# A two-layer decoder trunk on one core: the last expert quad in larger pieces with fillers, one early row block, and the residual through identity products

## The reference, cut to what matters

```
def hier_moe(h, w_group, b_group, w_expert, b_expert, w_in, w_out):
    ...
    def expert_block(args):
        xb, e = args
        hu = xb @ w_in[e]
        return (jax.nn.silu(hu[:, :EXPERT_FF]) * hu[:, EXPERT_FF:]) @ w_out[e]
    ...
```

## Time and profile before

| | |
|---|---|
| median of 3 runs | 1163.95 us (1163.62 to 1163.96) |
| profiled execution, its own time | 1165.64 us |
| its span, first to last instruction | 1163.8 us |
| mean granted PE clock | 0.865 |
| PE busy | 823.4 us, 71% of the span |
| DVE, ACT, POOL busy | 276.2, 140.6, 24.0 us |
| read from memory | 444.41 MB, 384 GB/s over the span |

### The profile page before, as it was taken

The page is one execution under the profiler, slowest core; times in us unless marked ns, Lnnn a source line. Parts: engine busy times, 40 slices in busy tenths (PEclk is TensorE's granted clock), DMA queues, the critical chain, the costliest instruction groups (busy, mean ns, idle before and its releaser), DMA issues.

```text
span 1163.8 us, 12340 instructions
## 1 busy us (share of the span) xinstructions
PE 823.4 (71%) x5238; PEld 403.2 (35%) x5238; DVE 276.2 (24%) x504; ACT 140.6 (12%) x328; POOL 24.0 (2%) x27
## 2 busy tenths in 40 slices
PE   9999999672727282818689999959191919190966
PEld 8965655130303030303234565613030303030322
DVE  3565673010101010101038746401010101010102
ACT  2011211010101010101012241101010101010100
POOL 1000110000000000000002100000000000000000
PEclk9999999895959595959789999989595959596989
DMA  9995398999999999999999818899999999999997
GB/s 351 274 330 214 152 389 344 429 432 425 435 423 430 429 433 427 433 425 426 416 416 405 346 71 344 336 429 432 427 431 427 435 424 432 427 433 427 425 419 286
DMA packets 46344, 447.74 MB, mean 385 GB/s; under 512 B 3632, under 2 KB 5976, under 8 KB 26072
## 3 DMA queue, kind: packets, MB, share of 16 engines
q1 hardware_dynamic: 44224, 444.42, 91.4%
q10 hardware_dynamic: 2072, 2.62, 1.2%
HBM read 444.41 MB, written 2.62 MB: 384 GB/s over the span
## 4 chain that ended last, share of the span: by engine, by line
PE 45%; DMA 43%; SPq 9%; issue 1%; DVE 1%; ACT 1%; POOL 0%; DVEq 0%; POOLq 0%
PE ps L1386 44%; DMA ring<-in_moe_w_in 40%; SPq L461 5%; SPq L378 4%; DMA spare<-in_moe_w_out 3%; PE ps L1389 1%; DMA xs<-in_x 0%; ACT ps L665 0%; DVE work L1133 0%; DVE ring L1265 0%; ACT work L661 0%; POOL rstd L518 0%; ACT work L608 0%; DVEq L65 0%; ACT work L753 0%
## 5 line engine op out<-in xcount | busy, mean ns | idle before, releaser
L1386 PE MATMUL ps<-ring,work 128*32 128x512 f32 (+1 forms) x2464 | 440.3, 651 | 298.3 <-DMA ring<-in_moe_w_in 286.8
L1386 PEld LDWEIGHTS ps<-ring,work 128*32 128x32 f32 (+1 forms) x2464 | 149.1, 132 | 564.6 <-issue 560.4
L1386 PE MATMUL ps<-work 128*32 128x512 f32 (+3 forms) x1170 | 214.1, 534 | 18.9 <-DVE work L1216 9.8
L1208 DVE SCALAR_TENSOR_TENSOR work<-work,ps 128x512 f32<-128x512 f32 x16 | 17.3, 1081 | 635.4 <-ACT work L691 635.4
L1386 PEld LDWEIGHTS ps<-work 128*32 128x32 f32 (+2 forms) x1170 | 88.5, 139 | 135.7 <-issue 111.3
L1386 PE MATMUL ps<-spare,work 128*32 128x512 f32 x256 | 117.1, 608 | 0.0
L691 ACT ACTIVATE work<-ps 128x512 f32<-128x512 f32 x16 | 17.5, 1097 | 539.3 <-PE ps L1386 539.3
L1386 PEld LDWEIGHTS ps<-work,xs 128*128 128x128 f32 x512 | 58.8, 192 | 15.1 <-issue 15.1
L1386 PE MATMUL ps<-work,xs 128*128 128x128 f32 x512 | 62.8, 279 | 0.0
L1386 PE MATMUL ps<-work,ring 128*128 128x128 f32 (+1 forms) x352 | 53.3, 313 | 0.3 <-DVE work L809 0.3
L1386 PEld LDWEIGHTS ps<-work,ring 128*128 128x128 f32 x352 | 49.3, 191 | 4.5 <-issue 0.6
(11 more groups left out here) (155 smaller groups left out, 353.2 us busy)
## 6 DMA issues: line engine op xcount, KB each, us to landing
ring<-in_moe_w_in SPq DMA_DIRECT2D x38, 4096.0 KB, 30.6
ring<-in_moe_w_in SPq DMA_DIRECT2D x44, 2048.0 KB, 14.2
work<-in_moe_w_out SPq DMA_DIRECT2D x42, 2048.0 KB, 34.8
spare<-in_moe_w_out SPq DMA_DIRECT2D x14, 2048.0 KB, 46.2
ring<-in_moe_w_in SPq DMA_DIRECT2D x16, 1024.0 KB, 30.3
ring<-in_hg_w_in SPq DMA_DIRECT2D x7, 2048.0 KB, 22.7
work<-in_moe_w_out SPq DMA_DIRECT2D x21, 512.0 KB, 17.6
ring<-in_w_kv SPq DMA_DIRECT2D x3, 2048.0 KB, 26.8
```

The costliest lines, as they stand in the source:

```text
L1208: dve.scalar_tensor_tensor(hid_rows, hid_rows, 1.0, in_hidden(6), ALU.add, ALU.mult).then_inc(silu_ready, 1)
L1386: return pe.matmul(o, l, r, start=start, stop=stop)
```

## The change

1. `load_last_up` has two pieces instead of three: row blocks 0 to 3 and 4 to 7. PE takes them so, with the 12 fillers after the first piece instead of after the second and third.
2. `load_last_down` has the pieces k 0 and 1, k 2, k 3 instead of four single k (in layer 1 the last is still cut into halves), and PE runs 12 fillers after the first and after the second piece.
3. After the up products of the last quad PE adds the residual to the four accumulators, by products of `ident` with it. At the end of a layer what is left is a copy of each accumulator: tile 0 by ACT (`sum_experts`, counted by the new `moe_summed`), tile 1 by DVE.
4. Row block 0 of the second quad's first expert is sent ahead, to `early` in region 5, after the last residual add and behind the opening loads; ACT copies it to its place in `ring` when PE has read the first quad's first row block. The refill's first part then has three experts. DVE waits for that copy before it writes in region 5.
5. `biasload` and `biasout` become one semaphore.

```diff
-ROW_PARTS = (1 + GRP, 2 + GRP)
+ROW_PARTS = (1 + GRP, 2)
+LAST_DOWN = (slice(0, 2), slice(2, 3), slice(3, 4))
...
+        early = rt[:, 896:1920]
...
+        def residual(layer, a, half):
+            if layer:
+                return x_rows[:, a, :, half * 64:(half + 1) * 64].rearrange("p k q -> p q k")
+            return x_rows[:, a, 4 * half:4 * half + 4, :].rearrange("p k q -> p q k")
...
@@ SP: load_opening, load_refill
+                    sp.wait_ge(x_added, 6 * (layer + 1))
+                    sp.dma_start(early, up_matrix(layer, GRP)[:, 0:D]).then_inc(early_in, 16)
...
-                        sp.dma_start(pairs[:, :, ns], source[:, :, ns]).then_inc(row_part_in[min(part, 1)], 16)
+                        xs = slice(0 if part else 1, GRP)
+                        sp.dma_start(pairs[:, xs, ns], source[:, xs, ns]).then_inc(row_part_in[min(part, 1)], 16)
...
@@ SP: the last quad
-                    for part, ks in enumerate(((0, 4), (4, 6), (6, 8))):
-                        if part == 1:
+                    for part, ks in enumerate(((0, 4), (4, 8))):
+                        if part:
                             sp.wait_ge(up_done, 2 * (P0 + QUADS - 1))
                         for x in range(GRP):
-                            load_pair(E - GRP + x, x, loaded[2 * x] if part == 2 else row_part_in[part], ks)
+                            load_pair(E - GRP + x, x, loaded[2 * x] if part else row_part_in[0], ks)
...
-                    parts = [(k, slice(0, D)) for k in range(KF)]
+                    parts = [(k, slice(0, D)) for k in LAST_DOWN]
                     if layer:
-                        parts[KF - 1:] = [(KF - 1, slice(0, 512)), (KF - 1, slice(512, D))]
+                        parts[-1:] = [(LAST_DOWN[-1], slice(0, 512)), (LAST_DOWN[-1], slice(512, D))]
...
@@ ACT: before the quads
+                act.wait_ge(early_in, 16 * (layer + 1))
+                act.wait_ge(first_k_done, 2 * layer + 1)
+                act.copy(pair(0)[:, 0:D], early).then_inc(early_moved, 1)
                 act.wait_ge(gat_done, 2 * P0 + 2)
                 weighted_columns(layer, 1, 1).then_inc(xg_ready, 2)
...
+            def sum_experts(layer, half):
+                act.wait_ge(c_done, 4 * (layer + 1) * QUADS - 3 + 2 * half)
+                if layer == 0:
+                    act.copy(x_rows[:, 0, 4 * half:4 * half + 4, :], ps[:, half, :].rearrange("p (q k) -> p k q", k=4))\
+                       .then_inc(moe_summed, 1)
+                else:
+                    act.copy(x_out[:, 0, half * 512:(half + 1) * 512], ps[:, half, :]).then_inc(moe_summed, 1)
...
@@ DVE
                 passes(layer)
+                dve.wait_ge(early_moved, layer + 1)
...
+                dve.wait_ge(c_done, 4 * (layer + 1) * QUADS - 2 + 2 * half)
+                if layer == 0:
+                    dve.tensor_copy(x_rows[:, 1, 4 * half:4 * half + 4, :], in_rows(ps[:, 2 + half, :])).then_inc(moe_added, 1)
+                else:
+                    dve.tensor_copy(x_out[:, 1, half * 512:(half + 1) * 512], ps[:, 2 + half, :]).then_inc(moe_added, 1)
...
@@ PE: the last quad
-                                for part, ks in enumerate((range(0, 4), range(4, 6), range(6, 8))):
-                                    if part < 2:
-                                        pe.wait_ge(row_part_in[part], 16 * ROW_PARTS[part] * (layer + 1))
+                                for part, ks in enumerate((range(0, 4), range(4, 8))):
+                                    if part == 0:
+                                        pe.wait_ge(row_part_in[0], 16 * ROW_PARTS[0] * (layer + 1))
                                     else:
                                         pairs_in()
...
-                                        if part == 2:
+                                        if part:
                                             i.then_inc(up_done, 1)
                                     if part == 0:
                                         i.then_inc(rows_done, 1)
-                                    if part:
                                         keep_busy(12, 5)
...
                             pe.wait_ge(xg_ready, it * (2 * UN) + (2 * q + 4))
+                        else:
+                            for a in range(TT):
+                                for half in range(2):
+                                    mm(ps[:, 2 * a + half, :], ident, residual(layer, a, half), False, False)
                         pe.wait_ge(hid_ready, it * UN + (q + 1))
...
-                        for k in range(KF - 1):
-                            pe.wait_ge(down_part_in[k], 16 * GRP * (layer + 1))
+                        for i, ks in enumerate(LAST_DOWN[:-1]):
+                            pe.wait_ge(down_part_in[i], 16 * GRP * (layer + 1))
                             for half in range(2):
-                                down(layer, down_home, half, [k])
-                        pe.wait_ge(down_part_in[KF - 1], 16 * GRP * (layer + 1))
+                                down(layer, down_home, half, range(KF)[ks])
+                            keep_busy(12, 5)
+                        pe.wait_ge(down_part_in[len(LAST_DOWN) - 1], 16 * GRP * (layer + 1))
                         down(layer, down_home, 0, [KF - 1]).then_inc(down_done, 1)
```

More of the change, by code:

```diff
@@ L192, in build @@
         ms_ready, rstd_ready, eps_added = sem("ms_ready"), sem("rstd_ready"), sem("ffn_eps_added")
-        x_added, moe_added = sem("residual_added"), sem("experts_added")
+        x_added, moe_added, moe_summed = sem("residual_added"), sem("tile1_experts_added"), sem("tile0_experts_added")
         row_part_in = [sem(f"row_part{i}_in") for i in range(2)]
-        down_part_in = [sem(f"last_down_part{k}_in") for k in range(KF)]
+        down_part_in = [sem(f"last_down_part{k}_in") for k in range(len(LAST_DOWN))]
         count_done = sem("counts_done")
@@ L447, in load_last_up @@
                 def load_last_up():
-                    for part, ks in enumerate(((0, 4), (4, 6), (6, 8))):
-                        if part == 1:
+                    for part, ks in enumerate(((0, 4), (4, 8))):
+                        if part:
                             sp.wait_ge(up_done, 2 * (P0 + QUADS - 1))
                         for x in range(GRP):
-                            load_pair(E - GRP + x, x, loaded[2 * x] if part == 2 else row_part_in[part], ks)
+                            load_pair(E - GRP + x, x, loaded[2 * x] if part else row_part_in[0], ks)
                 def load_last_down():
                     sp.wait_ge(down_done, 2 * (P0 + QUADS - 1))
-                    parts = [(k, slice(0, D)) for k in range(KF)]
+                    parts = [(k, slice(0, D)) for k in LAST_DOWN]
                     if layer:
-                        parts[KF - 1:] = [(KF - 1, slice(0, 512)), (KF - 1, slice(512, D))]
-                    for i, (k, cs) in enumerate(parts):
+                        parts[-1:] = [(LAST_DOWN[-1], slice(0, 512)), (LAST_DOWN[-1], slice(512, D))]
+                    for i, (ks, cs) in enumerate(parts):
                         for x in range(GRP):
-                            sp.dma_start(down_view(down_home[x])[:, k:k + 1, cs],
-                                         down_rows(moe_w_out[layer, E - GRP + x])[:, k:k + 1, cs])\
-                              .then_inc(down_in[x] if i == KF else down_part_in[i], 16)
+                            sp.dma_start(down_view(down_home[x])[:, ks, cs],
+                                         down_rows(moe_w_out[layer, E - GRP + x])[:, ks, cs])\
+                              .then_inc(down_in[x] if i == len(LAST_DOWN) else down_part_in[i], 16)
                 over_quads(sp, body, lambda: over(layer))
@@ L702, in moe @@
                 over_quads(act, body, lambda: over(layer))
+            def sum_experts(layer, half):
[5 more added lines that the diff above has]
+                    act.copy(x_out[:, 0, half * 512:(half + 1) * 512], ps[:, half, :]).then_inc(moe_summed, 1)
             moe(0)
+            for half in range(2):
+                sum_experts(0, half)
             act.wait_ge(down_done, 2 * QUADS)
@@ L779, in _ @@
             moe(1)
+            for half in range(2):
+                sum_experts(1, half)
         @block.vector
@@ L1360, in _ @@
             column_difference(MIX1 + 6, OUT_SUMS[1], out_quarter)
[L1361 removed]
+            dve.wait_ge(bias_moved, 2 * 16)
             for h in range(H + 1):
@@ L1785, in body @@
                                 if is_int(it, 0):
+                                    pe.wait_ge(early_moved, layer + 1)
                                     pe.wait_ge(row_part_in[0], 16 * (ROW_PARTS[0] * layer + 1))
@@ L1835, in columns_T @@
             def columns_T(half, a):
-                pe.wait_ge(moe_added, 2 * half + a + 1)
+                pe.wait_ge(moe_added if a else moe_summed, half + 1)
                 for k in range(4 * half, 4 * half + 4):
```

17 lines of the change are left out of this document (9 added, 8 removed).

## The result

The changed kernel takes **1177.55 us** (median of 4 runs, 1176.0 to 1177.71) against 1163.88 (1163.62 to 1163.96): ratio 1.0117, 95% interval 1.0104 to 1.013, so slower, and 0.55 us above the top of the forecast's range. The profiled execution took 1177.52 us (span 1175.7), 11.9 more than the one of before.

A forecast was written before the change was run, and what follows sets the result against it. An expert phase was taken to last as long as its weights' arrival plus PE's remaining work; 7.95 + 3.35 - 2.4 = +8.9 us gave 1174.5, less 1.7 for the median: 1172.8 us, range 1166.5 to 1177.

The forecast's parts named there:

- The mechanism: In each last quad, PE's work behind the last up weights, fillers included, sets the pace instead of the data.
- 27.3: Predicted microseconds from the last up weights to the last k in a last quad, a sum of seven PE terms.
- the term for the identity products: Last quad: four products adding the residual put at 5.6 us, between 3.70 and 6.9, by VectorE's add with steps.
- rival 2: Last quad: identity products cost 6.9 us by ACT's ratio, 1.3 more per layer, total 1175.4; chance 0.10.
- +8.9: Predicted net change in us: +7.95 second layer's end, +3.35 first layer, -2.4 for the early row block.
- dividing the final moves: End of layer 0: ACT takes two of four moves that followed each other on VectorE, put at -0.5 us.
- the 1.7 us taken off for the median: Final step: 1174.5 lowered to 1172.8 because the profiled execution of before lay 1.7 us above the median.
- 1: Rival, last quad: identity products cost 3.70 us as if read in sequence, 1.9 less per layer, 1169.0; chance 0.24.
- 3: Rival, last quad: clock stays up in PE's 7 us wait, 2.3 us less per layer, 1168.2; chance 0.10.
- 4: Rival, last quads: fillers and identity products stay inside waits, -8.3 us in total, 1155.6, faster; chance 0.09.
- 5: Rival, layer openings: the early row block brings nothing because the queue runs dry later, +2.4 us, 1175.2; chance 0.05.
- The sign: Whole kernel: the change makes it slower, chance 0.83, against 0.09 for faster and 0.08 for same.

The follow-up runs named there:

- e2: The changed kernel with the identity products reading the residual in sequence and the steps put on the accumulator's columns, same sum: 1170.95 us.
- e3: The changed kernel with no steps on either side of the identity products, so the residual is added to other columns: 1170.97 us.
- e9: The kernel before, unchanged, run again with one profiled execution: 1162.91 us.
- e10: The kernel before, unchanged, run once more with one profiled execution: 1164.03 us.
- e4: The kernel before with the early row block alone: 1161.89 us, ratio 0.9984.
- e5: The changed kernel without the two groups of fillers between the down pieces: 1164.97 us, ratio 1.0008.
- e8: The kernel before with the early row block and one group of 12 fillers per layer in the last quad's long wait: 1160.28 us.

## Why the prediction was right or wrong

**The mechanism was right.** PE's own work behind the last up weights became the bound, the fillers with it, without a wait for data. The clock was 0.50 when the up records began, as the text had it, and 1.00 from the identity products to the last k (585.80 to 605.50, and 1146.30 to 1166.00 in layer 1). In the recorded order, with the measured starts of layer 0 and layer 1: 64 up records 9.4 and 8.7 (put at 9.4); hidden rows 1.4 (1.2; the row of the identity products, 7.23 long, still runs in the first 0.2 of it); the first two k 3.6 (3.5); fillers 2.9, third k 1.85, fillers 2.9 (2.9, 1.75, 2.9). The chain came to 29.0 and 28.3 us for 27.3.

**The step that failed is the term for the identity products**: 5.6 us, by VectorE's add with steps, where PE took 7.05 and 7.0. That is rival 2's price (6.9, by ACT's ratio) and a little more; e2 and e3 show that the 512-byte steps of the moving operand are its cause. It makes +2.85 us, the bulk of the 3.0 by which the sum, +8.9, fell short of the +11.9 between the profiled executions. What remains is small and of both signs: dividing the final moves between ACT and DVE in layer 0 gave 0.1, not 0.5 (first sum to mark 5.12 before, 603.82 to 608.94, and 5.00 after, 608.45 to 613.45); the end of layer 1 became 0.5 shorter, not 0.3.

**The second step that failed is the last one**, the 1.7 us taken off for the median. The profiled execution of before lay above its median because its last k of layer 0, and to a small part the late k of layer 1, ran at the lower clock, as far as three executions show it (e9, e10). But the sum starts at the arrival of the last up weights, ahead of those blocks, and replaces them by a chain of PE's work at full clock. The changed kernel has no such block; its profiled execution and its median are 0.03 us apart. So the 1.7 had nothing to be taken from. 3.0 and 1.7 are the whole miss, 1172.8 to 1177.55.

**Rivals.** 1 falls as a forecast, and e2 shows what it would have been: 1169.0 in the text, 1170.7 without the 1.7 taken off, 1170.95 measured where its condition is brought about. 2 is the case that occurred (1175.4; with the 1.7 back, 1177.1). 3 falls: the clock read 0.50 when the second half began. 4 falls: its condition was the three costs together under 4.5 us, and they are 7 and 5.8. 5 falls: e4 gains 1.9. The early row block and the larger pieces together did what the text gave them, -1.3 and -1.8 to the arrivals where -1.6 each was put; in layer 0 three executions of the kernel before differ there by 0.7 (577.77 to 578.47), so one execution each fixes the split only roughly. The larger pieces can be read by themselves: from the start of the last quad to the arrival 20.00 us became 19.66 in layer 0 and 19.94 became 19.66 in layer 1, 0.3 of the 0.4 that was put. ACT's new copy (1.05 us) ended long before the work ahead of which it stands, and the gathered columns came at 186.82 for 186.59, as much later as the opening itself (0.23).

**The sign** hung on the 27.3, as the text said, and that sum was short, not long.

## What to carry to other kernels

Fillers cost nothing only in a wait that is longer than they are; once other work of the engine has filled that wait, they are the path, at their full price, and with no wait left there was no fall of the clock for them to prevent (e5). When products move a residual or any other operand into an accumulator, put the steps of a turned layout on the accumulator's side and let the moving operand run in sequence. And when a sum replaces a stretch of the trace, subtract nothing that only that stretch explains, such as the distance of its execution from the median.

## What the runs showed of the hardware that was not expected

- A float32 product whose moving operand has 512 bytes between neighbours took 1.95 times one in sequence on PE (7.23 against 3.70 us for four of 128 x 512); steps of 16 and 32 bytes on the accumulator's side took 3.70, no more than none.
- After one and the same wait of 3.19 us, in the same kernel, the last k of layer 0 ran in one execution at clock 0.50 and in another at full clock. With such falls in both layers an execution took 2.7 us longer than with none (1165.64 and 1162.91), on a kernel whose 18 executions beside e5 to e8 lay between 1161.61 and 1166.07. In a third (e10) it fell one k earlier: the third k ran behind a wait of 2.44 us, and its last records took 1.03 where the first took 0.63. Why the clock fell in one and not in the other, no run here shows.
